# A mixer block and a feed-forward block on one core: inversion steps between the parts of a dense gate product, rotary turns and norms moved, buffers laid out anew

## The reference, cut to what matters

```
proj = rms_norm(x) @ w_in
q, k, v = silu(conv5(proj[qkv]));  q = l2_norm(q) / sqrt(128);  k = l2_norm(k)
decay = exp(g_i - g_j), lower triangle;  m = strict(k_beta k^T * decay)
t_inv = inverse(I + m)
u = t_inv (v beta);  w = t_inv (k_beta exp(g));  a = tril(q k^T * decay)
scan over chunks: v_new = u - w S;  o = q exp(g) S + a v_new;  S = S exp(g_last) + k_dec^T v_new
sw = softmax(rotary(q_s) rotary(k_s)^T / 8 within 128, with a sink) v_s
mix = [rms_norm(o_fwd + o_bwd) * silu(z), sw * silu(sz)];  x = x + mix @ w_out
```

## Time and profile before

| | |
|---|---|
| time, median of 3 (lowest to highest) | 1098.31 us (1096.22 to 1100.35) |
| profiled execution, its own time | 1095.42 us |
| its span, first to last instruction | 1093.6 us |
| mean granted TensorE clock | 0.976 of full |
| busy in the span: TensorE | 1014.5 us (93%) |
| VectorE, ScalarE, GpSimd | 459.4, 448.7, 414.0 us |

### The profile page before, as it was taken

One profiled execution on the slowest core, in us unless ns is written; L12 is line 12 of the kernel. 1 busy time (PEld: TensorE's weight loads), 2 busy tenths in 40 slices (PEclk: granted clock), 3 DMA queues, 4 the chain that ended last, 5 costly groups with the idle time before them and its releaser, 6 DMA issues.

```text
span 1093.6 us, 12916 instructions
## 1 busy us (share of the span) xinstructions
PE 1014.5 (93%) x5326; PEld 839.0 (77%) x5326; DVE 459.4 (42%) x744; ACT 448.7 (41%) x800; POOL 414.0 (38%) x221
## 2 busy tenths in 40 slices
PE   5999779759999899979999999989999999999997
PEld 4887557647889898868777767878888888888876
DVE  5046922077666536240112263243333333474434
ACT  5356337724445226244234443244343434342223
POOL 2565325543002144353432323244443435354440
PEclk9999989869999999999999999989999999999999
DMA  7422212000000005332221101123323232322212
GB/s 258 149 61 83 69 58 78 1 0 1 1 1 1 1 1 183 119 115 76 78 77 59 58 1 58 58 96 99 115 79 114 81 112 83 110 96 96 96 38 77
DMA packets 22730, 80.41 MB, mean 74 GB/s; under 512 B 2480, under 2 KB 2736, under 8 KB 22544
## 3 DMA queue, kind: packets, MB, share of 16 engines
q1 hardware_dynamic: 21808, 77.95, 21.9%
q10 hardware_dynamic: 864, 1.64, 0.4%
HBM read 77.48 MB, written 2.10 MB: 73 GB/s over the span
## 4 chain that ended last, share of the span: by engine, by line
PE 78%; DVE 12%; ACT 7%; POOL 1%; issue 1%; DMA 1%; DVEq 0%; ACTq 0%
PE bank L1722 75%; PE bank L1730 3%; DVE qk L1332 2%; DVE swr L1326 1%; ACT L1044 1%; DVE vc L1332 1%; DVE xl L1326 1%; DVE dd L1326 1%; DVE xs L1332 1%; ACT ee L1044 1%; ACT qk L1044 1%; ACT xs L1044 1%; ACT wh L1044 1%; DVE mp L1326 1%; DVE r L1326 1%
## 5 line engine op out<-in xcount | busy, mean ns | idle before, releaser
L942 POOL TENSOR_TENSOR wl<-raw,wh 128x1024 fp32r<-128x1024 f32 (+1 forms) x131 | 315.3, 2412 | 472.2 <-ACT wh L1044 472.1
L1722 PE MATMUL bank<-xh,wh 128*128 128x512 f32 (+1 forms) x536 | 207.2, 387 | 8.7 <-DVE xl L1326 4.8
L1722 PE MATMUL bank<-xl,wh 128*128 128x512 f32 (+1 forms) x536 | 206.4, 385 | 0.0
L1722 PE MATMUL bank<-xh,wl 128*128 128x512 f32 (+1 forms) x536 | 206.3, 385 | 0.0
L1044 ACT ACTIVATE wh<-raw 128x1024 fp32r<-128x1024 f32 (+1 forms) x131 | 135.4, 1043 | 140.1 <-PE bank L1722 140.0
L1722 PE MATMUL bank<-wh,xh 128*128 128x512 f32 (+1 forms) x352 | 139.5, 396 | 16.6 <-DVE xl L1326 7.2
L1722 PE MATMUL bank<-wh,xl 128*128 128x512 f32 (+1 forms) x352 | 135.8, 386 | 0.0
L1722 PE MATMUL bank<-wl,xh 128*128 128x512 f32 (+1 forms) x352 | 135.7, 385 | 0.0
L1722 PEld LDWEIGHTS bank<-xh,wh 128*128 128x128 f32 x536 | 102.0, 190 | 30.3 <-issue 7.5
L1722 PEld LDWEIGHTS bank<-xh,wl 128*128 128x128 f32 x536 | 102.0, 190 | 19.7
L1722 PEld LDWEIGHTS bank<-xl,wh 128*128 128x128 f32 x536 | 102.0, 190 | 19.4
(11 more groups left out here) (224 smaller groups left out, 1507.6 us busy)
## 6 DMA issues: line engine op xcount, KB each, us to landing
raw<-in_wflat SPq DMA_DIRECT2D x127, 512.0 KB, 3.5
h<-in_x SPq DMA_DIRECT2D x4, 512.0 KB, 5.4
h<-in_x SPq DMA_DIRECT2D x1, 2048.0 KB, 8.7
gain<-in_pr SPq DMA_DIRECT2D x3, 512.0 KB, 3.7
consts<-in_cf SPq DMA_DIRECT2D x1, 1472.0 KB, 7.0
raw<-in_wflat SPq DMA_DIRECT2D x4, 272.0 KB, 3.3
out<-outt ACTq DMA_DIRECT2D x4, 256.0 KB, 2.1
out<-outt SPq DMA_DIRECT2D x4, 256.0 KB, 2.1
```

The lines of the kernel that those rows point to most:

```text
L942: e.tensor_tensor(WL[u % NS][:, 0:n], RAW[u % NS][:, 0:n], WH[u % NS][:, 0:n].bitcast(F32), ALU.subtract).then_inc(w_lo.up(u), 1)
L1722: return e.matmul(o, l, r_, start=start, stop=stop, skip_group_check=part)
```

## The change

1. **Channel stage.** One step of `swa_prep` follows every unit from 0 on, and none has two. The gates follow units 6 and 8. The thirteenth step, the rotary step of block 3, comes behind convolution 11.
2. **Gate stage.** The parts of both gates are ordered one by one. `rope_turn` is now first and `qk_norm` behind it, both among the parts of gate sz. After every second part of gate z stands one step of chunk 3 or chunk 0 by turns: two decays, `inv_kq` and `inv_m` for each, eight steps in all. The evacuation of a gate (`evac`) is put into the order behind its sixteenth part and what follows that, so z's stands behind `inv_m` of chunk 0.
3. **Between z and the attention.** Eight rounds: a transpose of v or k; a first step of chunk 1 (four rounds), then of chunk 2; and one of the next steps of chunk 0 or 3 by turns (`inv_mt`, `inv_x` 1, `inv_d` 1, `inv_x` 2). The transposes now use banks of the ring that starts with z's bank 0.
4. **Attention rounds.** As before, but chunks 0 and 3 enter with 8 steps done and 1 and 2 with 4.
5. **Buffers.** Tiles that would lie on the normalised input, which the dense products still read, are moved (`mp`, `at` of chunks 0 and 3; `sl`, `kt`, `vt`, `sqt`, `skt`, `pm`, `pmt`, `swo`, `ot`), and waits are changed to fit.

The diff, cut (left out: the scans' names for `kt` and `vt`, the table of step names, and unchanged lines):

```diff
@@ -253,16 +253,16 @@
     VC = zb("vc", [128, 4, 512], F32, 64)
-    KT = zb("kt", [128, 4, 512], F32, 72)
-    VT = zb("vt", [128, 4, 512], F32, 80)
-    SL8 = [zb(f"sl{j}", [128, 512], F32, 72 + 2 * j) for j in range(8)]
+    KT = [zb(f"kt{c}", [128, 512], F32, (12, 14, 16, 18)[c]) for c in range(4)]
+    VT = [zb(f"vt{c}", [128, 512], F32, (28, 30, 0, 2)[c]) for c in range(4)]
+    SL8 = [zb(f"sl{j}", [128, 512], F32, 32 + 2 * j) for j in range(8)]
     MIX = zb("mix", [128, 4, 1024], F32, 88)
...
     R2 = zb("r2", [128, 640], F32, 124.5)
-    SKT = zb("skt", [128, 512], F32, 127)
-    SQT = zb("sqt", [128, 4, 512], F32, 64)
+    SKT = zb("skt", [128, 512], F32, 128)
+    SQT = zb("sqt", [128, 4, 512], F32, 116)
     BD = small("bd", 64, [128, 4, 16])
@@ -283,8 +283,8 @@
 
-    MP = [zb(f"mp{c}", [128, 2, 512], F32, 4 * c) for c in range(4)]
-    AT = [zb(f"at{c}", [128, 2, 512], F32, 16 + 4 * c) for c in range(4)]
+    MP = [zb(f"mp{c}", [128, 2, 512], F32, (72, 4, 8, 76)[c]) for c in range(4)]
+    AT = [zb(f"at{c}", [128, 2, 512], F32, (80, 20, 24, 84)[c]) for c in range(4)]
 
@@ -298,10 +298,10 @@
     O = zb("o", [128, 4, 512], F32, 104)
-    PM = [zb(f"pm{i}", [128, 384], F32, 116 + 1.5 * i) for i in range(2)]
-    PMT = [zb(f"pmt{i}", [128, 384], F32, 119 + 1.5 * i) for i in range(2)]
-    SWO = zb("swo", [128, 512], F32, 122)
-    OT = zb("ot", [128, 512], F32, 129)
+    PM = [zb(f"pm{i}", [128, 384], F32, 64 + 1.5 * i) for i in range(2)]
+    PMT = [zb(f"pmt{i}", [128, 384], F32, 67 + 1.5 * i) for i in range(2)]
+    SWO = zb("swo", [128, 512], F32, 70)
+    OT = zb("ot", [128, 512], F32, 116)
     SCAN = [dict(VB=zb("vb0", [128, 512], F32, 32), KB_=zb("kb0", [128, 512], F32, 34), KD=zb("kd0", [128, 512], F32, 36),
@@ -552,53 +552,51 @@
                 do("square", j - 2)
-        if j in (1, 3):
+        step(g3)
+        if j in (6, 8):
             step(g2)
-        if j:
-            step(g3, 2 if j > 6 else 1)
     do("conv", 11)
...
             pass
-    G.over((0, 1, 2, 3))
-    g1 = in_turn(qk_norm(), to_tokens("v"), rope_turn(), to_tokens("k"))
-
-    def tok_part(u0, n, by, *sides):
+    G.over((4, 5, 6, 7))
+    BI.over((4, 5, 6, 7))
+    gi = [invert(cb) for cb in (0, 3, 1, 2)]
+    g1 = in_turn(rope_turn(), qk_norm())
+
+    def tok_parts(u0, name):
         ids, i = G.ids, G.i
...
         for tb in range(4):
-            G.take(("tok", u0, tb), by(tb))
+            G.take(("tok", u0, tb), (proj, (name, tb)))
         G.ids, G.i = ids, i
...
             w_ahead(u0 + k + 2)
-            do("tok", u0, k, "n0", SLOT0, n)
-            for g, m in sides:
-                step(g, m)
-
-    G.over((4, 5, 6, 7))
-    tok_part(U_SZ, 512, lambda tb: (proj, ("sz", tb)), (g1, 3))
-    gi = [invert(cb) for cb in (0, 3, 1, 2)]
-    BI.over((4,))
-    ids, i = G.ids, G.i
-    G.over((0, 1, 2, 3))
-    for tb in range(4):
-        G.take(("tok", U_Z, tb), (proj, ("z", tb)))
-    G.ids, G.i = ids, i
-    for k in range(4):
-        w_ahead(U_Z + k + 2)
-        do("tok", U_Z, k, "n0", SLOT0, 512)
-        step(g1, 4)
-        if k in (1, 2):
-            step(gi[0])
-    while step(g1):
-        pass
-    step(gi[1], 2)
+            for tb in range(4):
+                do("tok_b", u0, k, "n0", SLOT0, 512, tb)
+                yield
+        do("evac", u0)
+
+    n = 0
+    for _ in in_turn(tok_parts(U_SZ, "sz"), tok_parts(U_Z, "z")):
+        n += 1
+        if n <= 16:
+            step(g1, 2 if n <= 4 else 1)
+        elif n % 2 == 0:
+            step(gi[n // 2 % 2])
+    assert not step(g1)
+    BI.over((0, 1, 2, 3, 4, 5, 6, 7))
+    G.over((0, 1, 2, 3, 4))
+    g1 = in_turn(to_tokens("v"), to_tokens("k"))
+    for n in range(8):
+        step(g1)
+        step(gi[2 + n // 4])
+        step(gi[n % 2])
+    assert not step(g1)
     BI.over((0, 1, 2, 3, 4))
-    gs = swa()
     for b in (5, 6, 7):
         BANK[("swa", b)] = (b, emptied[b])
-    for g in gi[2:]:
-        step(g, 2)
+    gs = swa()
     live = True
@@ -1108,9 +1106,8 @@
             on.wait_ge(*tok_p.at((what, cb)))
-            on.wait_ge(*qk_g.at(6))
-            on.wait_ge(*qk_v.at(7))
-            act((VT if what == "v" else KT)[:, cb, :], psum[b][:, :], ACT.Copy, tok_a.up((what, cb)))
+            on.wait_ge(*dense.at((U_Z + 3, 3)))
+            act((VT if what == "v" else KT)[cb][:], psum[b][:, :], ACT.Copy, tok_a.up((what, cb)))
 
@@ -1139,13 +1136,13 @@
             on.wait_ge(*rope_p.at(i))
-            on.wait_ge(*tok_a.at(("v", 3)))
-            on.wait_ge(*tok_p.at(("v", 3)))
             act(SKT[:] if i == 4 else SQT[:, i, :], psum[b][:, :], ACT.Copy, rope_a.up(i))
...
         def tok(u0, i, which, ks, n):
-            if i < 3 or u0 in (U_OUT, U_OUT2):
-                return
+            if i == 3 and u0 not in (U_OUT, U_OUT2):
+                evac(u0)
+
+        def evac(u0):
             for tb in range(4):
@@ -1166,6 +1163,11 @@
             on.wait_ge(*gate_v.at("ngc"))
+            if cb == 0:
+                on.wait_ge(*qk_g.at(6))
+                on.wait_ge(*qk_v.at(7))
+            if cb == 3:
+                on.wait_ge(*rope_p.at(4))
             if cb in (1, 2):
@@ -1195,6 +1197,8 @@
                 on.wait_ge(*swa_p.at(("t", n - 2)))
+            else:
+                on.wait_ge(*tok_p.at(("v", 3)))
             act(PM[n % 2][:, 0:nk], psum[5][:, 0:nk], ACT.Exp, swa_a.up(("p", n)), bias=MX[:, qb, h:h + 1], scale=0.125,
@@ -1448,7 +1452,8 @@
             on.wait_ge(*inv_p.at(("q", cb)))
-            on.wait_ge(*dense.at((U_Z + 3, 3)))
+            if cb in (1, 2):
+                on.wait_ge(*dense.at((U_Z + 3, 3)))
             for d in range(2):
```

More of the change, by code:

```diff
@@ L1008, in scan_keys @@
             on.wait_ge(*tok_a.at(("v", cb)))
-            k3 = h3(KT[:, cb, :])
+            k3 = h3(KT[cb][:])
             if r:
                 e.tensor_tensor(h3(W["KB_"][:]), k3, b4r(BEG[:, d, cb, :]), ALU.mult).then_inc(scan_g.up(("kb", d, r)), 1)
-            e.tensor_tensor(h3(W["VB"][:]), h3(VT[:, cb, :]), b4r(BETA[:, d, cb, :]), ALU.mult).then_inc(scan_g.up(("vb", d, r)), 1)
+            e.tensor_tensor(h3(W["VB"][:]), h3(VT[cb][:]), b4r(BETA[:, d, cb, :]), ALU.mult).then_inc(scan_g.up(("vb", d, r)), 1)
             if r < 3:
@@ L1314, in scalar_engine @@
         return dict(begin=begin, prep=prep, stat=stat, split=split, conv=conv, square=square, qsum=qsum, qexp=qexp, to_tok=to_tok,
-                    gate1=gate1, gate2=gate2, rope_root=rope_root, rope_t=rope_t, tok=tok, inv_decay=inv_decay, inv_m=inv_m,
+                    gate1=gate1, gate2=gate2, rope_root=rope_root, rope_t=rope_t, tok=tok, evac=evac, inv_decay=inv_decay, inv_m=inv_m,
                     inv_d=inv_d, swa_s=swa_s, swa_t=swa_t, swa_o=swa_o, scan_keys=scan_keys, scan_v=scan_vn, scan_o=scan_o,
```

## The result

The changed kernel takes 1108.82 us (median of 4, 1108.17 to 1109.07), the kernel before in the same rounds 1097.26; the ratio is 1.0101, 95% interval 1.0077 to 1.0125. The change makes the kernel 1% slower. The time lies inside the range of 1088 to 1110, but not in the likeliest case (A, 1096 to 1106): it is the time of rival C.

What follows compares the result with a forecast made beforehand. TensorE was taken to bound most of the span, except the channel stage's end and the inversions' front. z's end +2.7 and the part behind it -0.5 gave +2.2 on 1098.3: about 1100.5 us, range 1088 to 1110.

Steps and rivals of the forecast that it cites:

- A: Whole kernel: time nearly equal to before, -3 to +7 us, 1096 to 1106; chance 0.48.
- rival C: Behind z: TensorE's work at half clock, streaming at +56 or later, 8 to 10 us longer, 1108; chance 0.24.
- the twelfth Copy: End of channel stage: ScalarE's Copy of unit 11 comes at 134.75 us, with 7.6 saved on units 7 to 10.
- release: Before the gate products: TensorE goes on at 143.2 us, after a rotary step slowed 4.65 us beside GpSimd's subtraction.
- the dense stretch: Gate products: no wait, net +5.1 us of work, last z product at 203.6 us, 2.7 later than before.
- The wait on z's Silu: Behind z, before v's first transpose: TensorE waits until +6.2 us for ScalarE's evacuation of z.
- k's copy: Between z and the attention: held behind ScalarE's rounding of chunk 1's factor, until +26.1 us.
- the drain: At ScalarE's table switches: about 1.38 us each by the skill's rule, left out; with it, about 1103 us.
- 19.2, so +45.3: Between z and the attention: chunk 2's steps and two levels of chunks 0 and 3 take 19.2 us, ending at +45.3.
- +48.3: Start of streaming, counted from the last z product, when the first attention scores go by; bounds 25 and 52.7.
- 1.5 for the clock's recovery: Streaming part: 1.5 us added to TensorE's 123.1 us of work for its clock to recover.
- B: Front of the inversions shrinks with its work, half of 28 us lost there stays away, 1087 to 1089; chance 0.25.

Runs made afterwards that it cites:

- experiment 4: Changed kernel plus sixteen fp32 products with unread results, placed in TensorE's waits behind z; 1105.47 us (1.0068).
- 1: Changed kernel with each of z's banks emptied by ScalarE right behind its own last part, not behind chunk 0's factor; 1105.34 us (1.0069).
- 2: Changed kernel with the norms ahead of the rotary turn among the parts of gate sz; 1103.76 us (1.0056).
- 7: Changed kernel with three edits together: z's banks emptied one by one, norms first, GpSimd's turn masks late; 1100.74 us (1.0035).
- 8: As 7, plus 16 attention steps among the last four rounds between z and the attention, inversions on banks 0 to 4; 1097.52 us (0.9987).
- 9: As 8, with norm and rotary steps begun only behind the fourth part of gate sz; 1086.89 us (0.9897).
- 5: Changed kernel with the channel stage back in its old order of gates and rotary steps; 1112.80 us (1.0142).
- 6: Changed kernel with the eight inversion steps of chunks 3 and 0 behind gate z, not among its parts; 1114.95 us (1.0159).
- 12: Changed kernel with only one edit: norm and rotary steps begun behind the fourth part of gate sz; 1114.61 us (1.0147).
- 3: Changed kernel with GpSimd's masks of the turned attention factor moved to level 3 of their chunk; 1108.24 us (1.0094).
- 11: As 9, with 24 attention steps instead of 16 among the rounds between z and the attention; 1086.04 us (0.9893).

## Why the prediction was right or wrong

**Right.** The channel stage: the twelfth Copy at 134.0 (134.75; 0.55 of the difference is that the first Copy already came at 61.41 and not at 61.96), release at 142.5 (143.2) by the rotary step that meets GpSimd's subtraction. In the dense stretch no wait was predicted and none came; z ended at 201.4, 2.2 better than 203.6. 0.7 of that is the release; the rest of the sum (+5.1 for the stretch) was 1.5 too large, I haven't traced which term. The wait on z's Silu 6.0 (6.2); chunk 1's mask at +12.3 (+12.1); GpSimd's chain to +24.4 (+24.8); k's copy at +25.6 (+26.1). Up to there the queue order alone gives the time. The table load costs 1.28 us and the next activation follows it directly, in both places on the path (205.49 and 206.79, and the rows below), so the drain was rightly left out:

```profile
211.71 1.28 ACT L1042 ACT_TABLE_LOAD   x1
213.00 0.63 ACT L1042 ACTIVATE ee<-ee 128x512 f32<-128x512 f32 x1
```

The Trainium skill (ScalarE: Activation LUTs, What ACT_TABLE_LOAD costs) would have added a drain of about 1.38 us to the switch; there is none between the two rows, and none ahead of the load, where the activation before it ends at 211.68.

**Wrong: the step "19.2, so +45.3".** It costed one level at half clock and the rest at full. The chain of the kernel after, over the same steps:

```profile
227.02 1.12 PE bank L1735 x4
228.13 3.32 PE bank L1727 x16
231.48 0.61 ACT dd L1042
232.13 1.97 PE bank L1735 x8
234.09 3.31 PE bank L1727 x16
237.40 0.87 PE bank L1735 x4
238.27 3.43 PE bank L1727 x16
241.72 1.29 DVE at L1330 x2
243.01 1.20 DVE xf L1330 x2
244.21 0.61 DVE mp L1330
244.89 1.28 POOL mp L978
246.19 3.41 DVE dd L1330 x2
249.60 0.61 DVE xf L1330
```

TensorE's six pieces are 14.0 us where my terms (0.7, 3.4, 0.6, 1.9, 3.0) made 9.6; VectorE and GpSimd are 8.4 where I had 8.3. The hand-overs were sized right, the work between them ran at half speed. The stretch behind it, up to the second score of the attention, took 4.7 us where I had 3.0, also at half clock (0.50 from 250 to 255); ScalarE's copies and the earlier start took some 0.8 less. So streaming began at +53.6 instead of +48.3: 5.3 late, and past the +53 from which C was to decide.

**Wrong: "1.5 for the clock's recovery".** From 255.0 to the last sum are 133.7 us, predicted 128.8 (123.1 + 1.5 + 1.8 + 2.4): 4.9 more. Half clock lasts from 255 to 265.8 (the row 265 to 270 has 0.92), and 10.8 us at half clock lose 5.4, not 1.5, which explains 3.9 of it.

**Missing: anything behind the last sum.** I carried the end over unchanged; low clock took 1.2 us in the scan and 1.5 near 490.

**The sum.** Predicted +2.2. With z's end -2.2, the middle +5.3, the streaming +4.9 and the rest +2.6 it makes 12.8, the measured growth of the span. Of the three positive terms, 4.4, 3.9 and 2.6 us, 10.9 together, are products that ran at half clock. Rival C had the cause, and its size (1108) in part by luck: it put the whole loss ahead of a streaming start at +56 or later, while the start came at +53.6 and over half of the loss behind it. I gave it 0.24 because I took the hand-overs as the term that decides; B was out, as no part of the front shrank. But "clock" is not the whole cause: experiment 4 took away over half of the time at half clock between 200 and 275 us and got back 3.4 of 11.6 us, while 1 and 2, which each only move a wait, got 3.5 and 5.1. Taking the three waits away (7) gives back 8.1 of the 11.6, and attention work in the front (8) 3.2 more. Waits and clock hang together here: the half clock follows the long waits, and a wait filled with real work gains twice (in 9 4.3 us by the wait and 2.0 by the clock). That the 22 us worked out behind experiments 5 and 6 are the turns and the attention pieces, and in which shares, is argued from them and not measured by itself; a version with v's turns left under the gate wasn't tried, since its buffers lie on the input that z still reads.

## What to carry to other kernels

A stage whose work is moved under a full engine doesn't shrink by that work if what remains is a chain through several engines: look at what fills its waits, and leave the filler (here the attention) where the chain is. Behind waits like those here (4.4 to 10.4 us) cost the following work at half clock until the clock of a neighbouring window shows it back; here 10.8 us of full load still ran so. Put independent work ahead of a known wait, in the waiting engine's own queue: one line in a loop brought the scan start 7.7 us earlier in experiment 9. In 12 the same line brought the streaming 4.0 earlier, and a fall of the clock 120 us later took it back; whether the fuller stretch of 9 protects from that, no run shows. And judge a version by its end: in 3 the scan started 3.2 us earlier and the end stayed, in 7 it started level with the kernel before and the end came 5.6 late, in 8 a start 8.3 earlier gave 2.5 at the end.

## What the hardware showed that I had not expected

- TensorE fell to half clock in the midst of full load, for 14 us behind waits of only 0.21 and 0.74 us (12), and that cost more than the edit had gained (6.1 against 4.0). The kernel after has the same two waits there (0.23 and 0.75) and kept its clock.
- Single episodes of about 1.5 us, in unchanged code at about 480, 570 and 590 us, are there in some traces (3 and 7 to 12; in 8 to 11 up to 16 us earlier, as the scan start is; the kernel after has the first of them, near 490) and not in that of the kernel before. Fast kernels have them too, 9 three (0.71, 0.68 and 0.71 at 465, 550 and 575 us); in experiment 7 they take most of the 5.8 us by which its end is late although its scan starts level. Experiment 8 has two groups of times 6 us apart, with mean granted clocks of 0.965 to 0.970 and of 0.958. What starts such an episode I can't say from these runs.
